# Sixteen gated-product buffers of two feed-forwards, laid 32 bytes further apart

## What is computed

```python
def conv_glu_ffn(xn, w_up, conv_w, conv_b, w_down):          # D_FF = 2752
    u, gt = split_cols(xn @ w_up, (D_FF, D_FF))
    u = causal_dwconv(u, conv_w, conv_b)                      # three taps along the positions
    return (jax.nn.silu(u) * gt) @ w_down

# first_block, for layer in range(2):
#   h = h + mixed @ w_mix_out[layer]
#   h = h + memory_cross_attention(rms_norm(h, ...), mem_n, ...)
#   h = h + conv_glu_ffn(rms_norm(h, norm_ffn_g[layer]), ffn_w_up[layer], ...)
```

## Time and profile before

| | |
|---|---|
| median of 3 runs | 3100.81 us (3100.66 to 3103.07) |
| the profiled execution | 3100.67 us, its span 3098.9 us |
| TensorE busy | 2997.8 us (97%), 17696 matmul records |
| VectorE busy | 1741.0 us (56%) |
| ScalarE busy | 1272.6 us (41%) |
| GpSimd busy | 318.4 us (10%) |
| TensorE's mean granted clock | 0.99 of 2.4 GHz |

### The profile page before, as it was taken

One profiled execution on the slowest core, in us unless ns is written; L12 is line 12 of the kernel. 1 busy time (PEld: TensorE's weight loads), 2 busy tenths in 40 slices (PEclk: granted clock), 3 DMA queues, 4 the chain that ended last, 5 costly groups with the idle time before them and its releaser, 6 DMA issues.

```text
span 3098.9 us, 41482 instructions
## 1 busy us (share of the span) xinstructions
PE 2997.8 (97%) x17696; PEld 2469.0 (80%) x17696; DVE 1741.0 (56%) x2154; ACT 1272.6 (41%) x1702; POOL 318.4 (10%) x285
## 2 busy tenths in 40 slices
PE   8988889999999999999999998999999999999999
PEld 5877678778888766778888775689998888878998
DVE  6444454547544775546544745676666453566665
ACT  5443333434322564433322545544444333344443
POOL 1010000100000100000000200124310000013240
PEclk9999999999999999999999999999999999999999
DMA  5341023223332311323332331233332222233331
GB/s 186 113 112 29 29 72 127 96 68 96 95 91 90 111 61 55 109 68 95 95 88 92 92 90 28 55 96 99 105 110 92 85 86 98 69 89 102 100 107 67
DMA packets 340104, 274.89 MB, mean 89 GB/s; under 512 B 28768, under 2 KB 308832, under 8 KB 339408
## 3 DMA queue, kind: packets, MB, share of 16 engines
q1 hardware_dynamic: 335552, 252.83, 27.3%
q0 software_dynamic: 4368, 19.41, 1.9%
HBM read 263.83 MB, written 8.39 MB: 88 GB/s over the span
## 4 chain that ended last, share of the span: by engine, by line
PE 87%; DVE 6%; ACT 5%; issue 2%; POOL 0%; DMA 0%; DVEq 0%; SPq 0%; ACTq 0%; POOLq 0%
PE ps L189 86%; ACT arena L203 2%; ACT whi L206 1%; DVE arena L212 1%; DVE arena L220 1%; DVE wlo L212 1%; PE ps L192 1%; DVE hT L212 1%; DVE xlo L220 0%; ACT L203 0%; POOL arena L212 0%; DVE sml L229 0%; ACT arena L206 0%; DVE split L212 0%; DMA arena<-in_x 0%
## 5 line engine op out<-in xcount | busy, mean ns | idle before, releaser
L189 PE MATMUL ps<-split,whi 128*128 128x512 f32 (+1 forms) x3008 | 888.2, 373 | 14.6 <-DVE hT L212 6.0
L212 DVE TENSOR_TENSOR wlo<-wraw,whi 128x2048 fp32r<-128x2048 f32 (+5 forms) x261 | 565.8, 2170 | 485.1 <-ACT whi L206 484.5
L189 PE MATMUL ps<-xhi,whi 128*128 128x512 f32 (+2 forms) x2040 | 765.4, 380 | 17.4 <-DVE xlo L212 7.1
L189 PE MATMUL ps<-xhi,wlo 128*128 128x512 f32 (+2 forms) x1984 | 741.9, 374 | 0.0
L189 PE MATMUL ps<-xlo,whi 128*128 128x512 f32 (+2 forms) x1944 | 730.1, 376 | 0.0
L189 PEld LDWEIGHTS ps<-split,whi 128*128 128x128 f32 x3008 | 548.8, 189 | 131.2 <-issue 25.0
L206 ACT ACTIVATE whi<-wraw 128x2048 fp32r<-128x2048 f32 (+5 forms) x261 | 457.0, 1754 | 337.6 <-PE ps L189 237.2
L189 PE MATMUL ps<-split,wlo 128*128 128x512 f32 (+1 forms) x1504 | 553.6, 368 | 0.0
L189 PEld LDWEIGHTS ps<-xhi,whi 128*128 128x128 f32 (+1 forms) x2040 | 381.8, 189 | 101.1 <-issue 14.4
L189 PEld LDWEIGHTS ps<-xhi,wlo 128*128 128x128 f32 (+1 forms) x1984 | 374.5, 189 | 69.1 <-issue 5.1
L189 PEld LDWEIGHTS ps<-xlo,whi 128*128 128x128 f32 (+1 forms) x1944 | 365.8, 188 | 68.4
(11 more groups left out here) (132 smaller groups left out, 2430.6 us busy)
## 6 DMA issues: line engine op xcount, KB each, us to landing
wraw<-in_ffn_w_up SPq DMA_DIRECT2D x128, 512.0 KB, 5.2
wraw<-in_odd_w_in SPq DMA_DIRECT2D x24, 1024.0 KB, 5.1
wraw<-in_ffn_w_gate SPq DMA_DIRECT2D x44, 512.0 KB, 3.9
wraw<-in_ffn_w_down SPq DMA_DIRECT2D x20, 1024.0 KB, 5.2
wraw<-in_ffn_w_down SPq DMA_DIRECT2D x24, 768.0 KB, 4.4
wraw<-in_xattn_wkv SPq DMA_DIRECT2D x16, 1024.0 KB, 5.7
wraw<-in_xattn_wq SPq DMA_DIRECT2D x8, 1024.0 KB, 5.1
wraw<-in_xattn_wo SPq DMA_DIRECT2D x8, 1024.0 KB, 5.2
```

The source lines that it names most:

```text
L189: return self.e.matmul(out, lhsT, rhs, start=start, stop=stop, skip_group_check=True)
L212: return self.e.tensor_tensor(out, a, b, op)
```

## The change

In `ffn`, the list of the sixteen buffers is built in a loop that takes 8 unused columns of the arena (32 bytes) behind each. Buffer n then begins at n x 1032 columns in place of n x 1024. The buffers behind them begin 128 columns, 512 bytes, further on; the last column in use goes from 18948 to 19076, where 23680 is the first that belongs to the norm. `swiglu0` and `swiglu1` have a function of their own (`folded`) and keep their buffers. The lists of instructions of all engines are the same before and after.

```diff
             norm.mid = (0, 0)
             nt = -(-F // P)
             at[0] = 0
-            hid = [als() for _ in range(16)]
+            hid = []
+            for n in range(16):
+                hid.append(als())
+                al(8)
             cb = [al(T + 2), al(T + 2)]
             tb = [al(T), al(T)]
             size = [min(P, F - n * P) for n in range(nt)]
```

## The result

The kernel with its sixteen buffers 32 bytes further apart took 3107.60 us, the median of 20 runs (3104.68 to 3109.62), against 3101.38 us for the kernel before, also 20 runs (3096.48 to 3106.12). Compared round by round the ratio is 1.0018, with a 95% interval of 1.0012 to 1.0025: slower by 5.6 us, between 3.7 and 7.8. That is a small loss, real, and by the ratio inside the 0.2% in which the prediction put it; by the two medians alone, 6.2 us apart, it lies on the 0.2% itself. The profiled execution of after took 3109.29 us, its span 3107.5.

What follows compares the result with a forecast made beforehand. TensorE's pace was taken to bound the feed-forwards: writes cost 0, 960 matmuls at 5.1 ns add 4.9 us to 3100.67, giving 3105.6, or 3105.7 us on the median's footing. Range for 8 in 10: 3100.4 to 3108.9 us.

Steps and rivals of the forecast that it cites:

- within 0.2%: Whole kernel: measured time less than 6.2 us from no change, between 3094.6 and 3107.0 us; chance 0.77.
- What bounds the kernel: Both convolved feed-forwards, 720.60 us: TensorE's own pace, about 2 us of waiting, so slower reads show and slower writes are hidden.
- Writes: ScalarE's copies and VectorE's subtractions into product buffers: keep 632 and 692 ns, cost 0 under TensorE's slack.
- Reads, the price: TensorE's matmuls reading buffers off place 0: 5.1 ns more each, mix1's rate, whatever the bytes; 960 matmuls, +4.9 us.
- the lower and the upper bound: Read cost in both feed-forwards: lower 960 x 4.2 = +4.0 us, upper 1056 x 5.5 = +5.8 us, place 0 included.
- Reads, the count: Down-projections of both feed-forwards: of 1056 matmuls, 96 read buffer 0 at place 0 as before, 960 elsewhere pay.
- picture of a recovery: TensorE after a wait: groups of three take 0.70, 0.69, 0.68 us until back in step; 32-byte moves come sooner than recovery.
- The mechanism: TensorE's moving operand and next weights interfere by some 5 ns a matmul, staying in step while every operand has the same place.
- Nothing changes: Rival: places don't matter to TensorE's reads, groups stay at 0.68 us; 3100.8 us, chance 0.22.
- Half of them matter: Rival: only places off a multiple of 64 bytes are slow, 528 matmuls, +2.2 to +2.9 us; 3103.3 us, chance 0.17.
- Each step costs more: Rival: the price hangs on the change of place, 352 steps at 0.02 to 0.03 us, 7.0 to 10.6 us; 3109.3, chance 0.12.
- The places free the reads: Rival: the 13.3 ns beside each matmul's columns come back, up to 14.1 us less; 3086.7 us, chance 0.06.

Runs made afterwards that it cites:

- mix1_placed: Kernel before with mix1's eight buffers of T + 3 columns made T + 64, so both mixed outputs stand at multiples of 256 bytes: 3097.52 us, ratio 0.9995.
- const32_64: Kernel before with product buffers all at 32, then all at 64 (ffn0), in steps of 64, then 128 bytes (ffn1): 3104.03 us, one run; constant 32: 5600 ns a block.
- shift_all: Kernel before with every array, weights, X and arena alike, beginning 32 bytes later: 3101.85 us against 3101.34, ratio 1.0002.
- shift_weights: Kernel before with only the split weight halves, and the small arrays behind them, 32 bytes later: 3146.70 us against 3101.34, ratio 1.0148.
- hi_lo_apart: Kernel before with high halves at place 0, low halves at 32 and 64 (ffn0), 128 and 256 (ffn1): 3105.2 us, one run; blocks 5560, 5569, 5493, 5440 ns.
- const256_step16: Kernel before with product buffers all at 256, then all at 16 (ffn0), in steps of 256, then 16 bytes (ffn1): 3103.37 us, one run.

## Why the prediction was right, and where it was not

**The time and its sign.** 3105.7 us was forecast, +4.9; the two feed-forwards grew by 5.45 us, the medians are 6.2 apart and the ratio says 5.6. The chances named "within 0.2%" as by far the likeliest, which it is by the ratio, if narrowly; 3107.60 itself lies above the 3107.0 from which the prediction called a time slower, and above the 3104.8 to 3106.6 that it gave its likeliest case. It lies in the wide range, 3100.4 to 3108.9. Of the 1.9 us that the forecast was too low, 0.6 are the median of before, which is 3101.38 over 20 runs and was 3100.81 over 3, and 0.7 are the price.

**What bounds the kernel.** Right. No engine but TensorE changed, TensorE waits 1.1 us in ffn0 in both versions, and all of the growth is in its busy time. Given that, a pace that changes by 2% in 1056 matmuls can only show whole.

**Writes.** Right: 632 and 692 ns again.

**Reads, the price.** The method was right and the term a little small. That one price holds "whatever the bytes" was wrong: constant places cost 2.2 ns a matmul at 64, 5.0 at 16 and 6.7 at the other places; after's eight places average out near the price of mix1, and no row had promised that. The one spot of before that showed such places gave 5.1 ns; the blocks of eight tiles pay 140 ns for 24 matmuls, 5.8 ns. mix1_placed confirms that the spot was slow for its places. Of the lower and the upper bound the upper one, 5.8 us for 1056 matmuls, was the nearer to the measured 5.45.

**Reads, the count.** Wrong in kind: 96 matmuls at place 0 were left out as free. They are not: the starts of the block at 864.82 us put the three matmuls of tile 0 at 234, 230 and 230 ns, and only the very first group of the down-projection, before anything had stood elsewhere, runs at 227. Here the prediction's picture of a recovery holds: behind the wait of the earlier trace rows and its like in ffn1, before needs 6 and 9 matmuls to come down to 227 ns, and tile 0 has only three. Its upper bound had allowed for it. The total, divided by 1056, gives 5.2 ns each, near to the first price; down-projections 1 and 2, with their waits and shorter blocks of six, were in part at the slower pace already, and had less to lose. They grew by 1.59 us for 336 matmuls, 4.7 ns each, where the first grew by 1.11 us for 192, 5.8 each.

**The mechanism.** The number was right by another cause than the one given, so it owes something to luck. This is the step that failed: "stay in step as long as every operand has the same place", and lose it where the place *changes*. const32_64 shows the opposite: eight buffers at one and the same place 32 make the slowest blocks measured. shift_all and shift_weights show what the place stood for: the distance between moving operand and weights. In before, weights, X and arena begin at the same distance from a multiple of 512, so a place in the arena *is* the distance to the weights, and no row could tell them apart. "Two streams that get in each other's way" is not contradicted, and not shown. Falling into step does occur, at distances 0 and 256; with 512 columns at a constant 32 the starts keep varying between 231 and 235 ns and never come down. So the prediction had the condition wrong, and would have said that 32 bytes on all buffers is free. That a change of place costs was right in part: it does at some distances (hi_lo_apart, low halves at 32 and 64) and does not at others (128, 256).

With the table of constants, after's block can be added up: places 0, 32, 64 to 224, with 160, which no run measured, taken like its neighbours, give a mean of (5440 + 5493 + 6 x 5600) / 8 = 5567 ns. Measured are 5580. By that sum 127 of the 140 ns are the distances and about 13 the changes between them. This split is worked out, not measured, and hi_lo_apart shows that the additive rule is not exact.

**The rivals.** "Nothing changes" fell by the timeline, and by the ratio. The Trainium skill, SBUF — State Buffer, section "Door 1: The DMA port swizzle", has lines of 16 bytes and a cost only for crossing to a new one; by that rule after would have cost nothing, and so would constant 16 and 32. They cost 5.0 and 6.7 ns a matmul (const256_step16, const32_64). "Half of them matter" fell twice: groups in after don't alternate, and 128 and 192 are multiples of 64 and cost the full 6.7 ns. "Each step costs more" came near in size: a group in after costs 17.5 ns more, where its dividing line was 17.6 and the forecast had 15. As a cause it fell with the constant places, which pay without a step, and with step 256, which is free; where a change does cost, it is 4 ns each (low halves at 32) to 7 ns (at 64) on the mean of the 16 changes of a block. "The places free the reads" was wrong for 512 columns: none of the places tried is below 226.7 ns. For 256 columns it is what the last runs found: up to 6.7 of the 13.3 ns beside the columns can be had back. The prediction read those rows for a constant, and did not ask whether the sign of the effect could depend on the width.

**What stays open.** Whether the weights that count are those of the same matmul or the next ones, which are being loaded meanwhile: in the down-projections both stand at one place. Why the distance counts, why modulo 256, why 64 is milder than its neighbours at 512 columns, what a change of distance costs and when, and why 192, dear at 512 columns, is the best at 256. No run looks inside TensorE. Only fp32r operands with 128 rows were measured, and of the narrow ones only those distances in the table.

## What to carry to other kernels

Where TensorE sets the pace and every operand of a matmul comes from one on-chip memory, the distance between the moving operand and the weights, modulo 256 bytes, is a thing to lay out on purpose: for 512 columns of fp32r keep it at 0, for 256 columns try 192 with products at one distance next to each other, and read the verdict from starts some 48 groups apart in a waitless stretch, where 1 ns a matmul is plain while the total hides it. When a pad or a small buffer is added anywhere ahead of others, check what it does to that distance; here a pad of 32 bytes before the weights alone costs 45.9 us. And where a trace has one spot that shows a price but several causes vary together there, take the price, and leave the cause open until one kernel varies each by itself.

## What the runs showed of the hardware that was not expected

- Matmuls of 512 columns of fp32r start 226.7 ns apart when moving operand and weights are 0 or 256 bytes apart (modulo 256), 231.7 at 16, 228.9 at 64 and 233.3 ns at 32, 96, 128, 192 and 224.
- The distance counts and not the address of either: all of them 32 bytes on leaves 5440 ns a block, the weights alone 32 bytes on makes it 5600.
- Matmuls of 256 columns behave the other way: 120.0 ns in before, all at distance 0, and 113.3 at 192 behind a product that is at 192 too. At 32, 128 and 224 they gain 1.4 to 2.4 ns.
- The slower pace that shows after a wait in before, gaps of 229 to 235 ns for 6 matmuls in ffn0 before 227, is of the size of that at a wrong distance, which in after does not end in the down-projections. That both have one cause is not shown.
